# Sliding attention with bias and sink in VectorE's extreme pass, and a last stage that weighs four row tiles on TensorE

## The chip, the cores and the metric

One NeuronCore of a Trainium2 chip runs the kernel; the other cores do nothing for it. The metric is the device time of one execution in microseconds. Engines by name: TensorE (PE, with its weight loads PEld), VectorE (DVE), ScalarE (ACT), GpSimd (POOL) and SyncE (SP), which issues most of the transfers.

## The reference

It computes one inference step of a one-layer encoder on 1024 prompt rows and 64 sample rows of width 1024, all in fp32. Cut to what matters here:

```python
def sink_attention(q, k, v, bias, sinks):                   # 8 query heads on 2 kv heads, 64 wide
    sc = einsum(q, k) * SCALE + bias                        # bias: -slope * |distance|, -inf outside the window
    m = maximum(max(sc, axis=-1), sink)
    e = exp(sc - m[..., None])
    pr = e / (sum(e, axis=-1, keepdims=True) + exp(sink - m)[..., None])
    return einsum(pr, v)

q_a, k_a, v_a, logf, q_b, k_b, v_b = project(rmsnorm(x))    # one input projection
o_a = forgetting attention (8 heads, causal);  o_b = sliding attention, window of 3 chunks of 64
x = x + concat(rmsnorm(o_a), rmsnorm(o_b)) @ w_out
h = rmsnorm(x)
y = x + sum over the 2 chosen of 32 experts: weight * (silu(h @ w_gate) * (h @ w_up)) @ w_down
return rmsnorm(y, g_final), and the new keys and values
```

## The kernel before

All work is laid out in row tiles of 128: eight of the prompt and one with the 64 sample rows, so NT = 9. Five engines run programs of their own, each in the order written down, and wait on semaphores. The stages follow each other: input projection (to about 254 us of the profiled execution), forgetting attention (260 to 411), sliding attention (412 to 500), output projection with routing (504 to 655), experts (660 to 872), last stage (872 to the end). fp32 products of the attention's scores and of the projections are made of three products of rounded parts (high and low halves).

**Sliding attention.** 36 steps n, nine tiles i for each of four groups g; a step handles one query tile of two heads (u = 0, 1) against up to two key tiles. TensorE's order in step n is: transposes of the probabilities n (`strans`), scores n+2 (`sqk`), weighted values n-1 (`spv`). `sqk` first writes the distance bias into the bank by a product of the identity with a bf16 table (`alibi`), and the sink's value into column 256 by a product of ones with a column that holds it in three bf16 parts; the score products accumulate on top. VectorE's order in a step is: copy of half of the transposed probabilities (`scopy`), extreme of n+2 (`smax`, one reduction over two heads and the sink column), scaling of output n-1 (`snorm`, reciprocal and product), then in some steps the low halves of the next group's queries (`s_low_q`) and of one eighth of w_out (L1282). ScalarE's order is: exponentials of n+1 read from PSUM (`sexp`), the other half of the copy, then in some steps the high halves of queries and w_out. GpSimd is idle here. A bank of scores is free for n+2 when the exponentials of n are done.

**Last stage.** When the last expert's rows lie in DRAM (`experts_done`), SP loads the final gain and then, for each of nine tiles, two 128x1024 blocks of expert rows (ya, yb; four slots). VectorE adds both with their weights to the residual in `o_all` (L1538, L1541), ScalarE makes the square sum and root (`norm_f`), VectorE the reciprocal and scaled output (`scale_f`, L1546, L1548) into one of two buffers (`fin`), and SP stores it. VectorE's order is add 0, add 1, scale 0, add 2, scale 1 and so on. SP's is: loads 0 to 3, then per tile i the load of i+4 (when add i is done) and the store of i. TensorE is idle, and GpSimd too.

Of the kernel before, what the change touches and what calls it, by code (L numbers as in the profile page):

```python
# [15 lines left out]
P = 128  # L16
D = 1024
# [28 lines left out]
def build(nc, t):  # L46

    ctx = ExitStack()
    with ctx:
# [52 lines left out]
        assert at + 8 * P <= free0 + 7 * D  # L102
# [34 lines left out]
        for name in ("den", "pg", "inv", "e21"):  # L137
# [6 lines left out]
        fin = [cut(big, free0 + 7 * D + u * D, D) for u in range(2)]  # L144
# [24 lines left out]

        ya = [cut(fox, 2 * WSLOT + u * D, D) for u in range(4)]  # L170
# [97 lines left out]
        sink_r = sinkp[:, 0:NH]  # L268
        sink_b, sink_1, sink_2 = (sinkp[:, NH + n * NH // 2:NH + (n + 1) * NH // 2].bitcast(BF16) for n in range(3))
# [31 lines left out]
            r_step r_exp r_mask r_mm r_id r_slot r_hot r_table id_init id_in v_ids  # L301
            pool_went idx_set dst_set g_done gT_done gT_cs gT_cv gu_done e_done ev_step hid_done hidT_done hidT_cp dn_done y_cs y_cv hg_set
            v_idx v_g v_w v_gT v_gTc v_gu v_e v_s v_hid v_hT v_hTc v_dn v_y v_out experts_done
            f_acc f_stat f_rms f_rstd f_fin f_out_a f_out_b""".split()
# [8 lines left out]
        y_in = [sem(f"y_in{u}") for u in range(4)]  # L313
# [65 lines left out]
        def scaled(g):  # L379

            return SCALE if g in (5, 6) else 1.0
# [13 lines left out]
        S_AT = {3: 0, 6: 1}  # L395
# [18 lines left out]
        def _(sp):  # L414
# [127 lines left out]
            sp.wait_ge(s["r_id"], 1)  # L542
# [55 lines left out]
            sp.dma_start(g1[:, :], row(t["g_final"], D)).then_inc(s["g_late_in"], 16)  # L598
# [5 lines left out]
            def store(i, u):  # L604
                sp.wait_ge(s["f_fin"], i + 1)
                sp.dma_start(t["y_prompt"].rearrange("a s d -> (a s) d")[ds(i * P, P), :], fin[u]).then_inc(s["f_out_b" if u else "f_out_a"], 16)
# [3 lines left out]
            for i in range(NT):  # L610
                if i + 4 < NT:
                    sp.wait_ge(s["f_acc"], i * 2 + 2)
                    load_y(i + 4, i % 4, P if i + 4 < SAMPLE else DEC)
                if i < SAMPLE:
                    store(i, i % 2)
            sp.wait_ge(s["f_fin"], NT)
            sp.dma_start(t["y_sample"].rearrange("a s d -> (a s) d"), fin[0][0:DEC, :]).then_inc(s["f_out_a"], 16)
            sp.wait_ge(s["f_out_a"], 16 * 5)
            sp.wait_ge(s["f_out_b"], 16 * 4)

        @block.gpsimd
        def _(pool):
# [22 lines left out]
            pool.iota(slots, [[1, P]], base=0, channel_multiplier=0, allow_small_or_imprecise_dtypes=True).then_inc(s["r_slot"], 1)  # L645
# [92 lines left out]
        def _(act):  # L738
# [141 lines left out]
            def s_high_q(g, part):  # L880

                a, b = PARTS[part]
                if g >= 2:
                    act.wait_ge(s["s_qk"], (g - 1) * NT)
                act.activation(sqh[g % 2][:, a:b, :], sq_raw[:, g, a:b, :], ACT.Copy, scale=SCALE).then_inc(s["s_hi"], 1)

            for n, (first, end) in enumerate(S_KEYS):
                s_high_k(n, first, end, 4 + n)
                if n < 2:
                    s_high_q(0, n)  # L890

            def sexp(n):
                lo = P if n % NT == 0 else 0
                act.wait_ge(s["s_nm"], n + 1)
# [17 lines left out]
            for n in range(NW):  # L912
# [4 lines left out]
                if i in S_AT and g < 3:  # L917
                    s_high_q(g + 1, S_AT[i])
# [101 lines left out]


# [15 lines left out]
            def norm_f(i, u, rows):  # L1037
                act.wait_ge(s["f_acc"], i * 2 + 2)
                if not (isinstance(i, int) and i < 2):
                    act.wait_ge(s["f_out_b" if u else "f_out_a"], (i - u) * 8)  # L1040
                act.activation(fin[u][0:rows, :], o_all[0:rows, ds(i, 1), :].rearrange("p a n -> p (a n)"), ACT.Square,
                               accum_out=st[0:rows, u:u + 1]).then_inc(s["f_stat"], 1)
                act.wait_ge(s["f_stat"], i + 1)
                act.activation(st[0:rows, 2 + u:3 + u], st[0:rows, u:u + 1], ACT.Sqrt, bias=eps[0:rows, 0:1], scale=1.0 / D).then_inc(s["f_rms"], 1)

            norm_f(0, 0, P)
            norm_f(1, 1, P)
            with act.Fori(1, NP_T // 2) as j:
                for u in range(2):
                    norm_f(j * 2 + u, u, P)  # L1050
            norm_f(8, 0, DEC)

        @block.vector
        def _(dve):
# [107 lines left out]
            def sink_step(n, ins):  # L1162
                ins.then_inc(s["s_aug"], 1)
                dve.wait_ge(s["s_aug"], n)

            pairs = sraw[:, :].rearrange("p (v g) -> p g v", v=2)
            by_pair = [a_.rearrange("p (g v) -> p g v", v=2) for a_ in (sink_1, sink_2, sink_r, sink_b)]
            sink_step(1, dve.tensor_copy(by_pair[0], pairs))
            sink_step(2, dve.tensor_tensor(by_pair[2], pairs, by_pair[0], ALU.subtract))
            sink_step(3, dve.tensor_copy(sink_2, sink_r))  # L1170
            sink_step(4, dve.tensor_tensor(sink_r, sink_r, sink_2, ALU.subtract))
            sink_step(5, dve.tensor_scalar(sink_b, sink_1, ident[:, 0:1], None, ALU.mult))
            sink_step(6, dve.scalar_tensor_tensor(out=sink_b, in0=sink_2, scalar=ident[:, 1:2], in1=sink_b, op0=ALU.mult, op1=ALU.add))
            sink_step(7, dve.scalar_tensor_tensor(out=sink_b, in0=sink_r, scalar=ident[:, 2:3], in1=sink_b, op0=ALU.mult, op1=ALU.add))

# [55 lines left out]
            def s_low_q(g, part):  # L1231

                a, b = PARTS[part]
                dve.wait_ge(s["s_hi"], sided(g, part))
                dve.scalar_tensor_tensor(out=sq_l[:, g, a:b, :], in0=sq_raw[:, g, a:b, :], scalar=SCALE, in1=sqh[g % 2][:, a:b, :].bitcast(F32),
                                         op0=ALU.mult, op1=ALU.subtract).then_inc(s["s_lo"], 1)

            for n, (first, end) in enumerate(S_KEYS):
                s_low_k(n, first, end, 4 + n)
                if n < 2:  # L1240
                    s_low_q(0, n)
# [28 lines left out]
            for n in range(NW):  # L1270
# [6 lines left out]
                if i in S_AT and g < 3:  # L1277
                    s_low_q(g + 1, S_AT[i])
                if n in WO_AT:
                    c = WO_AT.index(n)  # L1280
                    dve.wait_ge(s["wo_hi_set"], c + 1)
                    dve.tensor_tensor(w_out_l[:, c, :], fox[:, c * D + w_out_at:(c + 1) * D + w_out_at], w_out_h[:, c, :].bitcast(F32),  # L1282
                                      ALU.subtract).then_inc(s["wo_lo_set"], 1)
# [750 lines left out]
```

## Time and profile before

| | |
|---|---|
| time, median of 3 runs | 981.83 us (920.51, 981.83, 982.62) |
| the profiled execution: its own time, its span | 920.88 us, 919.0 us |
| mean granted TensorE clock | 0.940 |
| busy share PE, PEld, DVE, ACT, POOL | 87%, 75%, 49%, 36%, 12% |
| mean DMA rate | 136 GB/s |

The span runs from the first to the last instruction of the profiled execution; times of rows are microseconds from its start. Busy shares are means over stages with different limits, so each stage is read by itself.

### The profile page before, as it was taken

Reading aid. Unit: us, or ns where it says so; the run is one execution under the profiler, and the core shown is the slowest. Engines: PE = TensorE matmul, PEld = TensorE weight load, DVE = VectorE, ACT = ScalarE, POOL = GpSimd, SP = SyncE. Lnnn points to the kernel's source line nnn. Section 1 sums busy time; section 2 is a strip of 40 time slices with the busy share of each in tenths; the row PEclk is TensorE's granted clock in tenths of the full one; section 3 lists DMA queues with packets and bytes.
Section 4 is the critical chain, followed back from the end, with each engine's and each line's share of the span. In section 5 each row is a group of like instructions: output and inputs, shape, how many; then the busy total and the mean of one; then the engine's idle time right before and its main releaser. Section 6 shows DMA issues by size and latency. Waiting matters only on the chain.

```text
span 919.0 us, 15046 instructions
## 1 busy us (share of the span) xinstructions
PE 798.8 (87%) x5519; PEld 690.5 (75%) x5519; DVE 448.6 (49%) x1107; ACT 326.8 (36%) x811; POOL 111.0 (12%) x167
## 2 busy tenths in 40 slices
PE   3999999999969898899997999997499999999600
PEld 3999999999947676678997788886377777777400
DVE  4741111111056566656786447555356544544368
ACT  5631111112146566556775433322122222222123
POOL 0000000000021412000000000001223443343100
PEclk9999999999979999998998899999599999999955
DMA  9211411321350211005002312211699999972196
GB/s 276 72 56 47 139 50 46 69 67 49 82 113 6 61 36 29 1 21 210 2 2 85 149 50 88 69 58 67 222 401 406 362 331 341 336 287 83 47 388 216
DMA packets 68851, 124.63 MB, mean 136 GB/s; under 512 B 21787, under 2 KB 41075, under 8 KB 68787
## 3 DMA queue, kind: packets, MB, share of 16 engines
q1 hardware_dynamic: 59571, 105.91, 33.4%
q0 software_dynamic: 9216, 17.85, 5.3%
q8 instruction: 43, 0.70, 0.3%
q14 instruction: 21, 0.17, 0.1%
HBM read 108.72 MB, written 30.73 MB: 152 GB/s over the span
## 4 chain that ended last, share of the span: by engine, by line
PE 74%; DVE 9%; DMA 7%; ACT 5%; issue 3%; SPq 1%; POOLq 0%; DVEq 0%; ACTq 0%
PE ps L1580 30%; PE ps L1909 11%; PE ps L1915 5%; PE ps L1793 4%; PE ps L1686 4%; PE ps L1670 4%; PE ps L1902 3%; PE ps L1769 2%; DMA work<-c_rows 2%; ACT big L837 2%; PE ps L1701 2%; PE ps L1780 2%; DMA work<-in_w_in 2%; PE ps L1848 2%; DVE big L1186 1%
## 5 line engine op out<-in xcount | busy, mean ns | idle before, releaser
L1580 PE MATMUL ps<-xh,wg_lo 128*128 128x384 f32 (+1 forms) x288 | 94.7, 329 | 0.0
L1580 PE MATMUL ps<-xh,wg_hi 128*128 128x384 f32 (+1 forms) x288 | 93.9, 326 | 0.0
L1580 PE MATMUL ps<-xl,wg_hi 128*128 128x384 f32 (+1 forms) x288 | 93.8, 326 | 0.0
L1909 PEld LDWEIGHTS ps<-fox,work 128*128 128x128 f32 x320 | 60.6, 190 | 19.5 <-issue 12.3
L1909 PE MATMUL ps<-fox,work 128*128 128x256 f32 x320 | 72.5, 379 | 2.1 <-DVE work L1478 2.1
L1478 DVE COPY work<-ps 128x512 f32<-128x512 f32 x32 | 22.1, 692 | 91.6 <-PE ps L1902 91.5
L1686 PE MATMUL ps<-cf,big 128*128 128x128 f32 x312 | 49.6, 285 | 16.9 <-ACT big L837 15.3
L1580 PE MATMUL ps<-w_out_h,oTl 128*128 128x512 f32 x144 | 58.5, 407 | 1.5 <-DVE oTl L1321 1.5
L837 ACT ACTIVATE big<-big,nm 128x384 f32<-128x384 f32 (+7 forms) x72 | 54.1, 753 | 11.1 <-DVE nm L1186 10.8
L1081 DVE TENSOR_SCALAR fox<-ps 128x256 f32<-128x256 f32 (+2 forms) x21 | 10.2, 486 | 96.8 <-PE ps L1580 96.8
L1580 PE MATMUL ps<-w_out_h,oTh 128*128 128x512 f32 x144 | 56.8, 395 | 0.0
L1580 PE MATMUL ps<-w_out_l,oTh 128*128 128x512 f32 x144 | 56.8, 394 | 0.0
L1686 PEld LDWEIGHTS ps<-cf,big 128*128 128x128 f32 x312 | 35.3, 143 | 26.4 <-ACT big L837 21.5
L1580 PEld LDWEIGHTS ps<-xl,wg_hi 128*128 128x128 f32 x288 | 54.1, 188 | 0.0
L1580 PEld LDWEIGHTS ps<-xh,wg_lo 128*128 128x128 f32 x288 | 54.1, 188 | 0.0
L1580 PEld LDWEIGHTS ps<-xh,wg_hi 128*128 128x128 f32 x288 | 54.1, 188 | 0.0
L764 ACT ACTIVATE fox<-ps 128x256 f32<-128x256 f32 (+2 forms) x21 | 9.2, 436 | 96.7 <-PE ps L1580 96.7
L984 ACT ACTIVATE big<-ps 128x128 f32<-128x128 f32 x32 | 8.9, 277 | 96.7 <-PE ps L1909 96.7
L900 ACT ACTIVATE big<-ps,nm 128x257 f32<-128x257 f32 (+1 forms) x72 | 32.7, 461 | 24.5 <-DVE nm L1248 24.5
L1580 PE MATMUL ps<-wg_hi,xl 128*128 128x256 f32 x144 | 40.9, 284 | 0.2 <-DVE wg_lo L1077 0.2
L1580 PE MATMUL ps<-wg_lo,xh 128*128 128x256 f32 x144 | 40.8, 283 | 0.0
L1580 PE MATMUL ps<-wg_hi,xh 128*128 128x256 f32 x144 | 40.8, 283 | 0.0
(313 smaller groups left out, 1879.2 us busy)
## 6 DMA issues: line engine op xcount, KB each, us to landing
fox<-in_w_gate SPq DMA_DIRECT2D x20, 512.0 KB, 5.1
fox<-in_w_up SPq DMA_DIRECT2D x20, 512.0 KB, 12.2
fox<-in_w_down SPq DMA_DIRECT2D x20, 512.0 KB, 12.6
fox<-y_rows SPq DMA_DIRECT2D x16, 512.0 KB, 6.4
work<-in_w_in SPq DMA_DIRECT2D x6, 1024.0 KB, 5.6
h_rows<-big SPq DMA_DIRECT2D x9, 512.0 KB, 2.6
work<-in_x_prompt SPq DMA_DIRECT2D x8, 512.0 KB, 4.4
fox<-in_w_out SPq DMA_DIRECT2D x1, 4096.0 KB, 13.4
```

Source lines behind the costliest of these rows:

```text
L837: act.activation(prob[u][:, 0:w], prob[u][:, 0:w], ACT.Exp, bias=nm[:, 2 * (n % 2) + u:2 * (n % 2) + u + 1], scale=-1.0, accum_out=rs[:, 2 ...
L900: act.activation(sprob[n % 2][:, u, lo:2 * P + 1], ps[n % 2][:, 512 * u + lo:512 * u + 2 * P + 1], ACT.Exp, bias=nm[:, 2 * (n % 2) + u:1 + ...
L1478: dve.tensor_copy(hgT[u][:, 4:8, :], bank[1].rearrange("p (c k) -> p c k", c=4)).then_inc(s["gT_cv"], 1)
L1580: mm = pe.matmul(out, xs[a](c), ws[b](c), start=(c + k == 0), stop=(c == C - 1 and k == 2))
L1670: mm = pe.matmul(ps[u][:, at_:at_ + (m1 - m0) * P], q, key, start=(k == 0 and at_ // 512 != own // 512), stop=(k == 2), skip_group_check=True)
L1686: mm = pe.transpose(bank[b][:, (m % 4) * P:(m % 4) * P + P], prob[u][:, m * P:(m + 1) * P], ident)
L1701: mm = pe.matmul(bank[6][u * DH:u * DH + DH, 0:P], v, probT[u][n % 2][:, b * P:(b + 1) * P], start=(b == 0), stop=(b == nblk[i] - 1), skip ...
L1769: mm = pe.matmul(bank[2 * (n % 2) + u][:, at_:at_ + (m1 - m0) * P], q, key, start=False, stop=(k == 2), skip_group_check=True)
L1793: mm = pe.matmul(bank[6][:, (n % 2) * P + v * DH:(n % 2) * P + (v + 1) * DH], sprobT[n % 2][:, (2 * v + b) * P:(2 * v + b + 1) * P], val, ...
L1902: mm = pe.transpose(bank[c // 4][:, (c % 4) * P:(c % 4) * P + P], src[:, c, :], ident)
L1909: mm = pe.matmul(bank[2 + u][:, 0:2 * FE].rearrange("p (m f) -> p m f", m=2), hgT[u][:, c, :], wv[:, c, :, :], start=(c == 0), stop=(c == ...
L1915: mm = pe.matmul(bank[4 + n], ex["hidT"][u], w[:, 2 * D + 512 * n:2 * D + 512 * n + 512], start=True, stop=True)
```

## The change

In the sliding stage, `sqk` no longer puts bias and sink into the bank; the scores alone are made there. `smax` becomes two passes, one per head, each of which computes -(score + bias) into a buffer of SBUF (`sscore`) and, in the same pass, its minimum with the negated sink. `sexp` reads this buffer with scale -1, one head at a time; the sink is a column of it, copied in the first two steps of each group. A bank is free after the passes. Queries are scaled where they leave the projection. Halves of the queries of groups 1 to 3 and w_out's low halves move to GpSimd. In the last stage, tiles 1, 3, 5 and 7 are weighed on TensorE: diagonal matrices of the weights times ya and yb are summed in PSUM and VectorE adds the result once. Outputs have four buffers, squares one of their own, and the final gain is loaded while the experts run. SP waits with a slot's next load until the matmuls have read it.

```diff
+        squares = cut(swa, 0, D)
+        ON_PE = [1, 3, 5, 7]
+        diag = cut(swa, 5 * D, 2 * len(ON_PE), P)
+        fin = [cut(swa, D + u * D, D) for u in range(4)]
...
-        S_AT = {3: 0, 6: 1}
+        S_AT = {1: 0, 3: 1}
...
             gate_up(NSLOT, 0)
+            sp.wait_ge(s["hT_done"], 2 * NT)
+            sp.wait_ge(s["h_out_a"], 16 * 5)
+            sp.wait_ge(s["h_out_b"], 16 * 4)
+            sp.dma_start(g_fin, row(t["g_final"], D)).then_inc(s["g_late_in"], 16)
...
             for i in range(NT):
                 if i + 4 < NT:
-                    sp.wait_ge(s["f_acc"], i * 2 + 2)
+                    if i in ON_PE:
+                        sp.wait_ge(s["f_mm"], ON_PE.index(i) + 1)
+                    else:
+                        sp.wait_ge(s["f_acc"], i * 2 + 2)
                     load_y(i + 4, i % 4, P if i + 4 < SAMPLE else DEC)
+                store(i)
...
+            def side_piece(g, part):
+                a, b = PARTS[part]
+                hi = sqh[g % 2][:, a:b, :]
+                pool.tensor_copy(hi, sq_raw[:, g, a:b, :]).then_inc(s["s_hi"], 1)
+                pool.wait_ge(s["s_hi"], sided(g, part))
+                pool.tensor_tensor(sq_l[:, g, a:b, :], sq_raw[:, g, a:b, :], hi.bitcast(F32), ALU.subtract).then_inc(s["s_lo"], 1)
+            def low_out(c):
+                pool.wait_ge(s["wo_hi_set"], c + 1)
+                pool.tensor_tensor(w_out_l[:, c, :], fox[:, c * D + w_out_at:(c + 1) * D + w_out_at], w_out_h[:, c, :].bitcast(F32),
+                                   ALU.subtract).then_inc(s["wo_lo_set"], 1)
+            for n in range(NW):
+                g, i = n // NT, n % NT
+                if i in S_AT and g < 3:
+                    pool.wait_ge(s["s_qk"], n + 1)
+                    side_piece(g + 1, S_AT[i])
+                if n in WO_AT:
+                    low_out(WO_AT.index(n))
...
-                act.wait_ge(s["s_nm"], n + 1)
                 for u in range(2):
-                    act.activation(sprob[n % 2][:, u, lo:2 * P + 1], ps[n % 2][:, 512 * u + lo:512 * u + 2 * P + 1], ACT.Exp,
-                                   bias=nm[:, 2 * (n % 2) + u:1 + 2 * (n % 2) + u],
+                    act.wait_ge(s["s_nm"], 2 * n + u + 1)
+                    act.activation(sprob[n % 2][:, u, lo:2 * P + 1], sscore[n % 2][:, u, lo:2 * P + 1], ACT.Exp,
+                                   bias=nm[:, 2 * (n % 2) + u:1 + 2 * (n % 2) + u], scale=-1.0,
...
+            for k, i in enumerate(ON_PE):
+                for c in range(2):
+                    last = act.activation(diag[:, 2 * k + c, :], ident, ACT.Copy, scale=wgt[:, c * NT + i:c * NT + i + 1])
+                last.then_inc(s["f_diag"], 1)
...
-                dve.tensor_reduce(nm[:, 2 * (n % 2):2 * (n % 2) + 2], ps[n % 2][:, :].rearrange("p (u n) -> p u n", u=2)[:, :, lo:2 * P + 1],
-                                  AX.X, ALU.max, negate=True).then_inc(s["s_nm"], 1)
+                if i < 2:
+                    dve.tensor_copy(sscore[n % 2][:, :, 2 * P], neg_sink[:, 2 * g:2 * g + 2])
+                for u in range(2):
+                    a0 = g * 512 + u * 256
+                    dve.tensor_tensor_reduce(sscore[n % 2][:, u, lo:2 * P], bank[2 * (n % 2) + u][:, lo:2 * P], alibi[:, a0 + lo:a0 + 2 * P],
+                                             -1.0, neg_sink[:, 2 * g + u:2 * g + u + 1], ALU.add, ALU.min,
+                                             nm[:, 2 * (n % 2) + u:2 * (n % 2) + u + 1]).then_inc(s["s_nm"], 1)
...
             def add_y(i, j, u, rows):
+                if i in ON_PE:
+                    k = ON_PE.index(i)
+                    dve.wait_ge(s["f_mm"], k + 1)
+                    dve.tensor_tensor(o_all[0:rows, i, :], ps[k][0:rows, :], o_all[0:rows, i, :], ALU.add).then_inc(s["f_acc"], 2)
+                    return
...
                 if n >= 2:
-                    pe.wait_ge(s["s_exp"], 2 * (n - 1))
+                    pe.wait_ge(s["s_nm"], 2 * (n - 1))
-                for u in range(2):
-                    out = bank[2 * (n % 2) + u]
-                    a0 = g * 512 + u * 256
-                    pe.matmul(out[:, lo:2 * P], identb, alibi[:, a0 + lo:a0 + 2 * P], start=True, stop=False, skip_group_check=True)
-                for u in range(2):
-                    pe.matmul(bank[2 * (n % 2) + u][:, 2 * P:2 * P + 1], onesb, sink_b[:, 2 * g + u:2 * g + u + 1],
-                              start=False, stop=False, skip_group_check=True)
...
+            def weigh_y(k, i):
+                pe.wait_ge(s["f_diag"], k + 1)
+                pe.wait_ge(y_in[i % 4], Y_BASE[i % 4] + i // 4 * 32 + 32)
+                for n in range(2):
+                    cols = slice(512 * n, 512 * n + 512)
+                    pe.matmul(ps[k][:, cols], diag[:, 2 * k, :], ya[i % 4][:, cols], start=True, stop=False)
+                    mm = pe.matmul(ps[k][:, cols], diag[:, 2 * k + 1, :], yb[i % 4][:, cols], start=False, stop=True)
+                mm.then_inc(s["f_mm"], 1)
+            for k, i in enumerate(ON_PE):
+                weigh_y(k, i)
```

The seven small instructions that split the sinks into bf16 parts (L1168 to L1174, before the forgetting attention) become one that negates them.

## Rows read from the trace of the kernel before

**Rows 1.** The page: chain that ended last, share of the span by engine.

```profile
PE 74%; DVE 9%; DMA 7%; ACT 5%; issue 3%; SPq 1%; POOLq 0%; DVEq 0%; ACTq 0%
```

**Rows 2.** Chain of waits, 408 to 506 us: shares by line; one step (start us, us, what).

```profile
by line: PE ps L1793 36.4%; PE ps L1769 21.5%; PE ps L1780 16.5%; PE ps L1753 8.3%; PE ps L1817 2.0%; PE ps L1701 1.9%; DVE skl L1228 1.5%; DVE big L1296 1.5%; issue 1.4%; DVE sq_l L1235 1.4%; PE ps L1734 1.1%; PE ps L1755 1.0%; PE ps L1710
...
447.51 0.44 PE ps L1780 x4
447.95 0.22 PE ps L1753 x2
448.20 0.55 PE ps L1769 x6
448.75 1.03 PE ps L1793 x8
```

**Rows 3.** Groups of the sliding stage, 416 to 499 us.

```profile
L1248 DVE TENSOR_REDUCE nm<-ps 128x2 f32<-128x514 f32 x32 | 22.1, 690 | 12.3 <-PE ps L1769 12.3
...
L1256 DVE COPY big<-ps 128x256 f32<-128x256 f32 x32 | 13.3, 416 | 0.0
...
L1265 DVE TENSOR_TENSOR big<-ps,rc 128x128 f32<-128x128 f32 x35 | 10.2, 292 | 9.5 <-PE ps L1793 9.0
L1282 DVE TENSOR_TENSOR w_out_l<-fox,w_out_h 128x1024 fp32r<-128x1024 f32 x8 | 9.7, 1216 | 0.0
...
L1261 DVE RECIPROCAL rc<-rs 128x2 f32<-128x2 f32 x36 | 5.6, 155 | 0.0
```

**Rows 4.** Busy time of 440 to 452 us: PE, PEld, DVE, ACT, POOL; clock, DMA share, GB/s.

```profile
440.00:452.00 12.00, 12.00 (x117) 11.03 (x116) 9.96 (x26) 8.86 (x29) 0.00 (x0) 1.00 0.00 1
```

**Rows 5.** Groups of VectorE in the forgetting attention (260 to 411 us), and of GpSimd.

```profile
L1186 DVE CUSTOM_DVE_ANT_0 big<-ps,work 128x1024 f32<-128x1024 f32 x4 | 4.9, 1220 | 2.7 <-PE ps L1670 2.7
...
L1186 DVE CUSTOM_DVE_ANT_0 big<-ps,work 128x256 f32<-128x256 f32 x4 | 1.7, 422 | 1.3 <-PE ps L1670 1.2
...
L635 POOL TENSOR_TENSOR q_l<-fox,qh 128x640 fp32r<-128x640 f32 x3 | 4.7, 1550 | 0.2
...
L635 POOL TENSOR_TENSOR q_l<-fox,qh 128x512 fp32r<-128x512 f32 x3 | 3.8, 1272 | 0.2
```

**Rows 6.** Chain of waits, last stage (868 us to the end).

```profile
872.18 0.34 SPq L598
...
873.04 6.15 DMA fox<-y_rows
...
879.30 1.30 DVE big L1538
...
886.27 1.21 DVE big L1538
...
888.90 1.29 DVE big L1548
890.19 1.21 DVE big L1538
...
914.38 1.28 DVE big L1548
```

**Rows 7.** Busy time by stretch, last stage; last columns: granted clock, DMA share, GB/s.

```profile
868.00:872.00 4.00, 0.00 (x0) 0.00 (x0) 0.00 (x0) 0.00 (x0) 0.86 (x1) 0.66 0.15 57
...
876.00:878.00 2.00, 0.00 (x0) 0.00 (x0) 0.00 (x0) 0.00 (x0) 0.00 (x0) 0.50 1.00 410
...
902.00:904.00 2.00, 0.00 (x0) 0.00 (x0) 1.96 (x2) 0.98 (x2) 0.00 (x0) 0.50 1.01 262
```

**Rows 8.** Chain of waits: routing's end and the experts' start.

```profile
644.85 3.62 PE ps L1848 x16
...
664.93 8.43 PE ps L1909 x32
...
674.35 1.72 PE ps L1915 x4
676.07 3.45 PE ps L1909 x16
```

More of the change, by code:

```diff
@@ L101, in build @@
         sprobT = [cut(big, at + u * 4 * P, 4 * P) for u in range(2)]
-        assert at + 8 * P <= free0 + 7 * D
+        at += 8 * P
+        sscore = [cut(big, at + u * 2 * (2 * P + 8), 2, 2 * P + 8) for u in range(2)]
+        at += 4 * (2 * P + 8)
+        assert at <= free0 + 7 * D
         xr = [cut(big, free0 + u * D, D) for u in range(2)]
@@ L142, in build @@
         assert at <= free0 + 6 * D
-        fin = [cut(big, free0 + 7 * D + u * D, D) for u in range(2)]
+        g_fin = cut(big, free0 + 2 * D, D)
         fox, fox_at = sb_at("fox", [P, NT * QKV + WSLOT])
@@ L267, in build @@
         sinkp = sb("sinkp", [P, 4 * NH])
-        sink_r = sinkp[:, 0:NH]
-        sink_b, sink_1, sink_2 = (sinkp[:, NH + n * NH // 2:NH + (n + 1) * NH // 2].bitcast(BF16) for n in range(3))
+        neg_sink = sinkp[:, 0:NH]
         sraw = sb("sraw", [P, NH])
@@ L312, in build @@
         y_out = [sem(f"y_out{u}") for u in range(4)]
-        y_in = [sem(f"y_in{u}") for u in range(4)]
+        f_out = [sem(f"f_out{u}") for u in range(4)]
+        y_in, Y_BASE = x_in, [48, 32, 32, 32]
         x_rows = t["x_prompt"].rearrange("a s d -> (a s) d")
@@ L602, in load_y, with store @@
                 sp.dma_start(yb[u][0:rows, :], y_dram[ds(i * P + TOK, rows), :]).then_inc(y_in[u], 16)
-            def store(i, u):
+            def store(i):
+                rows = t["y_prompt"].rearrange("a s d -> (a s) d")[i * P:(i + 1) * P, :] if i < SAMPLE else t["y_sample"].rearrange("a s d -> (a s) d")
                 sp.wait_ge(s["f_fin"], i + 1)
-                sp.dma_start(t["y_prompt"].rearrange("a s d -> (a s) d")[ds(i * P, P), :], fin[u]).then_inc(s["f_out_b" if u else "f_out_a"], 16)
+                sp.dma_start(rows, fin[i % 4][0:P if i < SAMPLE else DEC, :]).then_inc(f_out[i % 4], 16)
             for i in range(4):
@@ L611, in _ @@
                 if i + 4 < NT:
-                    sp.wait_ge(s["f_acc"], i * 2 + 2)
+                    if i in ON_PE:
+                        sp.wait_ge(s["f_mm"], ON_PE.index(i) + 1)
+                    else:
+                        sp.wait_ge(s["f_acc"], i * 2 + 2)
                     load_y(i + 4, i % 4, P if i + 4 < SAMPLE else DEC)
[L614 to L619, printed above, removed]
+                store(i)
+            for u in range(4):
+                sp.wait_ge(f_out[u], 16 * len(range(u, NT, 4)))
         @block.gpsimd
@@ L1034, in _, with norm_f @@
             act.wait_ge(s["experts_done"], 1)
-            def norm_f(i, u, rows):
+            def norm_f(i):
+                u, rows = i % 2, P if i < SAMPLE else DEC
                 act.wait_ge(s["f_acc"], i * 2 + 2)
[L1039 to L1042, printed above, removed]
+                act.activation(squares[0:rows, :], o_all[0:rows, i, :], ACT.Square, accum_out=st[0:rows, u:u + 1]).then_inc(s["f_stat"], 1)
                 act.wait_ge(s["f_stat"], i + 1)
+                if i >= 2:
+                    act.wait_ge(s["f_rstd"], i - 1)
                 act.activation(st[0:rows, 2 + u:3 + u], st[0:rows, u:u + 1], ACT.Sqrt, bias=eps[0:rows, 0:1], scale=1.0 / D).then_inc(s["f_rms"], 1)
-            norm_f(0, 0, P)
-            norm_f(1, 1, P)
-            with act.Fori(1, NP_T // 2) as j:
-                for u in range(2):
-                    norm_f(j * 2 + u, u, P)
-            norm_f(8, 0, DEC)
+            norm_f(0)
+            for i in range(NT):
+                if i + 1 < NT:
+                    norm_f(i + 1)
         @block.vector
@@ L1160, in _ @@
                 flow(piece)
[L1162 to L1174, printed above, removed]
+            dve.tensor_scalar(neg_sink.rearrange("p (g v) -> p g v", v=2), sraw[:, :].rearrange("p (v g) -> p g v", v=2), -1.0, None,
+                              ALU.mult).then_inc(s["s_aug"], 1)
             def fmax(n, u):
@@ L1276, in _ @@
                     snorm(n - 1)
[L1277 to L1283, printed above, removed]
             snorm(NW - 1)
@@ L1768, in sqk @@
                                 key = swa_h[rows, m0:m1, 0:P]
-                            mm = pe.matmul(bank[2 * (n % 2) + u][:, at_:at_ + (m1 - m0) * P], q, key, start=False, stop=(k == 2),
-                                           skip_group_check=True)
+                            mm = pe.matmul(bank[2 * (n % 2) + u][:, at_:at_ + (m1 - m0) * P], q, key,
+                                           start=(k == 0 and at_ == spans[0][0]), stop=(k == 2), skip_group_check=True)
                 mm.then_inc(s["s_qk"], 1)
```

52 lines of the change are left out of this document (24 added, 28 removed).

## The prediction

> **What bounds the kernel now.** I read the chain of waits of the whole span first [rows 1]: TensorE holds 74% of it and VectorE 9%. The change touches two stages, so I read each by itself. The sliding stage runs from 411.75 to 499.7 us. Its chain [rows 2] is TensorE alone: one of its 36 steps is 0.44 us of transposes (L1780), 0.22 of bias (L1753), 0.03 of sink (L1755, seen only in the row by line), 0.55 of scores (L1769) and 1.03 of weighted values (L1793), 2.27 us in all, and a window of it has TensorE busy 12.00 of 12.00 us at full clock, VectorE 9.96 and ScalarE 8.86 [rows 4]. So here only what leaves TensorE shortens anything. In the last stage TensorE does nothing and VectorE runs without a gap: two weighted sums and a scaling per tile, 3.91 us from one tile to the next (886.27 to 890.19), first sum at 879.30, last scaling from 914.38 to 915.66 [rows 6]. But the DMA engines are full too, 410 GB/s from 876 us on and still saturated at 902 to 904 [rows 7]. A saving on VectorE there has little room before transfers end last.
>
> **Sliding stage: bias and sink leave TensorE.** By the row by line, L1753 holds 8.3% and L1755 1.0% of the 98 us window [rows 2]: 8.1 + 1.0 = 9.1 us, all on the path. The sink's one-column products overlap their neighbours, so their price is the 0.03 us a step, not their durations. Score matmuls stay as they are. A step becomes 2.27 - 0.25 = 2.02 us.
>
> Cover for this is VectorE. Each step had one 128x514 reduction, 0.69 us [rows 3]; now it has two 128x256 passes that add bf16 bias to PSUM and take the extreme. The nearest row is the forgetting attention's pass of that size, 0.42 us [rows 5], there with an fp32 second input. So a step of VectorE is 0.42 (copy) + 2 x 0.42 + 0.16 (reciprocal) + 0.29 (scaling of output) [rows 3] = 1.71 us, under 2.02 even before the overlap that back-to-back instructions show. The eight low-half subtractions of 1.22 us (L1282) leave its queue as well. Nothing late is created in order either: VectorE's order is copy n, extreme n+2, scaling n-1. With time 0 at a step's first transpose, scores n+2 end at 0.99, passes at 1.9, scaling n-1 at 2.4; TensorE asks for that scaling only at 3.0. Exponentials n+2 start after the first pass, at 1.5, take 2 x (0.47 + 0.2), and are wanted at 4.04. ScalarE loses its query halves and keeps w_out's high halves. It now reads scores from SBUF instead of PSUM, and a score bank is free after the pass instead of after the exponential; both only loosen. Bounds of this edit: if a pass with the bf16 input costs 0.42 us, -9.1 us. With overlap of the first steps, which run at half clock and where bias costs 0.43 us and the exponential waits less, another -1. If it cost up to 0.57 us, still the full gain. I take -9.5 us, bounds -11 and +5 (first rival).
>
> GpSimd takes what left the others: per group two casts and subtractions (1.27 us for 128x512, 1.55 for 128x640 [rows 5]) and eight 128x1024 subtractions. From those rows each further 128 columns cost 0.28 us, so 128x1024 is an estimated 2.4 us. Queries of the next group begin at step 1 of a group and are wanted at step 7, 12 us later, with at most two 2.4 us subtractions queued in front; the last w_out piece follows step 29, 12 us before the output projection wants it. Cost nothing; if that cover were gone, a late piece would stop TensorE for its 2.4 us.
> Eight small VectorE copies of the sink column are SBUF to SBUF. The Trainium skill (SBUF — State Buffer, section "SBUF: two separate sides") says that a VectorE copy in a two-port mode and a GpSimd instruction exclude each other for a whole instruction. No row of before shows such a pair; by it each copy that meets a w_out subtraction would wait up to an estimated 2.4 us. Six of the eight stand where GpSimd waits for the same scores or has finished, so I leave the sum as it is.
> Seven small sink instructions before the first forgetting pass vanish; the pass waits for the c_rows transfer anyway. Nothing. The earlier load of the final gain (0.5 MB) enters SP's queue behind an expert whose successors are loaded seven experts ahead, and its added waits are for stores that end before gathers start. Nothing.
>
> **Last stage.** Three effects, each against before's 879.30.
> (a) Gain not loaded here: SP's issue of 872.18 is gone and the rows' is 0.39 us earlier, and 0.5 MB less ahead of the first tile at 410 GB/s, 1.3 us. First sum at 877.6: -1.7 us.
> (b) Four tiles need one add from PSUM, by the nearest row (the extreme pass of 128x1024, 1.22 us, or L1538's 1.21) about 1.2 us, in place of 2.48: -1.28 each, -5.1 us in all. Floor of VectorE's work: 9 x 1.43 + 5 x 2.48 + 4 x 1.2 = 30.1 us instead of 35.2.
> (c) What TensorE needs. Tile 1's rows land one tile's 1.05 MB after tile 0's, 2.56 us, at 880.1, just when VectorE ends tile 0. Weighing is four fp32 matmuls of 512 columns. L1915 has two in 1.72 us at full clock [rows 8], so 3.45 us. But TensorE has been idle since 866; the window 868 to 872 already has 0.66 and the later ones 0.50 [rows 7], the 1.2 GHz level, where it is 6.9 us. How soon does the clock come back? The burst L1848 of 3.62 us stayed at half; at the expert stage's start 32 matmuls took 8.43 us where two times 3.45 is full speed, 1.53 us more, so it rose 3.1 us into them and 7.8 after the first transpose [rows 8]. Between those I take 6.1 us, bounds 5.0 and 6.9. In VectorE's order this add stands before tile 0's scaling, so tiles 0 and 1 are both held: +6.1 us.
> Behind it SP's order bites: it issues tile 5's load only after store 0, that is after tile 0's scaling at 888.9. Store and load are 1.5 MB, 3.8 us, plus some 2 us of latency: tile 5 lands at 895, TensorE is cold again (4.5 us idle; the mean of 0.66 puts the earlier drop at 869.3, 3 us after the last matmul), weighs until 900.4 to 901.9, and VectorE wants it at 899.3: +1.8 us. Tiles 3 and 7 are in time (890 against 892.8; 906 against 907.7). The final scaling waits as before.
> Sum: 877.6 + 30.1 + 6.1 + 1.8 + 0.5 for the last statistics = 916.1 against 915.7: +0.4 us; bounds -3 and +3. The diagonals (8 ScalarE copies of 128x128) run while the last scatter lands: nothing. Four output buffers instead of two remove ScalarE's waits on stores, which stopped nobody: VectorE has no gap in [rows 6].
>
> **Sum.** The profiled execution took 920.88 us, span 919.0. 920.9 - 9.5 + 0.4 = 911.8 us, 1.0% less. The timed runs shown are 920.51, 981.83 and 982.62; their median lies 61 us above the profiled one, and the profile shows nothing of those 61 us. I carry the difference of 9.1 over to the median: 981.8 - 9.1 = 972.7 us. Two of three runs lie at that level, so a median of three falls there more often than not, about 6 in 10; otherwise it is about 912.
>
> **Rivals**, each as a difference to before and at both levels.
> 1. VectorE becomes the bound of the sliding stage. If the pass with a bf16 bias costs over 0.70 us instead of 0.42, VectorE's step exceeds 2.27 and the stage gets longer than before: the decision point is (2.27 - 0.87)/2. At 0.77 us: 36 x (2.41 - 2.27) = +5, with the last stage +5.4: 926.3, at the median's level 987. For it: no row has this type. Against: fp32 passes and bf16 matter not to the cadence of any VectorE row shown. 8%.
> 2. The last stage keeps its saving, since the clock returns at once and tile 5 is early: +6.1 becomes 3.5 and +1.8 nothing, -4 there: 907.4 or 968. 15%.
> 3. The exclusion of the ports named above decides: say all eight copies wait 2.4 us; a step's slack on VectorE of 0.3 us absorbs little, 8 x 2.1 = +17 us, gain gone: 929 or 990, slower. For it: both engines are now busy together. Against: the order of their triggers, as worked out. 3%.
> 4. The stall in (c) is repeated: TensorE is cold for all four tiles, each late by 2 to 3 us: +6 instead of +0.4: 917.4 or 978, no change by measure. 14%.
> 5. The sliding stage's own waits eat half of its gain (TensorE behind GpSimd or exponentials): -4.5: 917 or 977. 12%.
> My own case: 48%.
>
> **How the numbers follow.** Predicted 972.7. The likeliest case's own range is 969 to 977, or 908 to 916 at the other level. The range must reach over both levels, since the level of the median is not decided by the change: low end 905 (rival 2 at the lower level), high end 982 (rivals 4 and 5 with the bounds of the stage); outside are rivals 1 and 3 and some scatter. 2% (18 us) is about what a measurement here can tell; all cases but rival 3 and the ends lie within it. Faster by over 2% needs the stage's full -11 and the last stage's -7 or more: 8%; slower, rival 3 and mishaps of that size: 7%.
>
> **What would show it.** In the sliding stage's chain no matmul with a bf16 bias, steps of 2.02 us, TensorE still busy throughout, passes near 0.42 us and an end of the stage about 9 us earlier. In the last stage: first sum at some 38.5 us before the end as before, VectorE idle some 6 us before the first PSUM add, a granted clock of 0.5 when TensorE's first weighing starts, store 0 some 2.5 us later than before. Wrong would be: TensorE waiting for the exponential in steady state, or VectorE's adds finding f_mm already set.

## The result, and the profile after

The changed kernel takes 972.77 us, the median of 971.13, 972.04, 973.51 and 974.34. Before takes 920.51, 925.01, 981.83 and 982.62 in the same comparison. Before has two levels of time, some 922 and some 982 us, and the changed kernel was seen on one only; the ratio of 1.054 (1.049 to 1.060) sets it against before's lower level. It is slower there by 5.4%. Against before's upper level it is 1% faster. So the question is what the two levels are, and why the changed kernel was seen on only one of them.

First the page of the changed kernel: the totals, the granted clock by slices of 24.2 us, the chain by engine, two groups.

```profile
span 969.3 us, 14926 instructions
PE 866.9 (89%) x5407; PEld 733.7 (76%) x5407; DVE 441.9 (46%) x1199; ACT 332.7 (34%) x813; POOL 142.1 (15%) x187
...
PEclk9999999999889999965555599999679999999976
...
PE 78%; DVE 7%; DMA 7%; ACT 4%; issue 3%; SPq 1%; POOLq 0%; DVEq 0%; ACTq 0%
...
L1810 PE MATMUL ps<-swa,big 128*128 128x64 f32 x256 | 64.3, 426 | 0.0
...
L1273 DVE CUSTOM_DVE_ANT_0 big<-ps,cb,sinkp 128x256 f32<-128x256 f32 (+1 forms) x72 | 30.9, 466 | 27.8 <-PE ps L1786 27.8
```

The clock row has a hole of six slices (6 5 5 5 5 5), which is the sliding stage from its start to its end. Before's page, profiled at the lower level, has 8 or 9 there:

```profile
PEclk9999999999979999998998899999599999999955
```

The same stage in the chain of waits of the changed kernel, in order of time. L1797 is the transposes (L1780 of before), L1786 the scores (L1769), L1810 the weighted values (L1793):

```profile
by line: PE ps L1810 49.4%; PE ps L1797 28.4%; PE ps L1786 27.7%
...
494.86 0.85 PE ps L1797 x4
495.71 0.94 PE ps L1786 x5
496.65 1.90 PE ps L1810 x8
```

Bias and sink are gone, as intended, and the chain is TensorE alone, as in [rows 2]. But a step takes 0.85 + 0.94 + 1.90 = 3.69 us where I had 2.02 and before had 2.27: each part lasts nearly twice as long as the same part in [rows 2]. The windows tell why; the columns are those of [rows 4], the last three the granted clock, the DMA share and GB/s.

```profile
416.00:420.00 4.00, 2.67 (x17) 1.79 (x16) 3.01 (x15) 2.14 (x9) 1.89 (x2) 0.74 1.03 422
420.00:422.00 2.00, 2.00 (x12) 1.45 (x11) 1.25 (x6) 1.36 (x5) 0.14 (x1) 0.50 1.01 403
422.00:424.00 2.00, 2.00 (x12) 1.67 (x14) 1.52 (x7) 1.37 (x5) 1.92 (x2) 0.50 1.04 414
...
440.00:452.00 12.00, 12.00 (x60) 10.44 (x61) 5.64 (x28) 5.98 (x20) 4.18 (x3) 0.50 0.00 1
```

In [rows 4] TensorE is busy 12.00 of 12.00 us at a granted clock of 1.00 (2.4 GHz); here it is just as busy, at 0.50 (1.2 GHz), with 60 matmuls instead of 117 (before's 117 include the bias and sink products). In both kernels the clock falls near the start of the stage. In the changed kernel it falls at about 417.9 us, behind waits of 1.45 and 1.18 us for the halves of keys and queries. In the profiled execution of before it had fallen at about 411.9 us, during the transposes of the keys, ahead of its waits (0.82 and 0.50 us). There it comes back between two neighbouring microseconds, which no group of rows ahead of the prediction shows:

```profile
421.00:422.00 1.00, 1.00 (x8) 0.83 (x7) 0.28 (x1) 1.00 (x5) 0.00 (x0) 0.50 1.02 410
422.00:423.00 1.00, 1.00 (x11) 0.85 (x10) 0.48 (x1) 0.25 (x1) 0.00 (x0) 0.94 1.03 410
```

In the changed kernel it stays at 0.50 until the output projection. The stage, from the first transpose of the keys to the end of the last scaling, runs from 412.74 to 546.64 us, 133.9 us instead of 87.9 (411.75 to 499.69). The last scaling in the chain of each, first the changed kernel, then before:

```profile
546.34 0.30 DVE big L1291
```

```profile
499.39 0.30 DVE big L1265
```

The last stage, in the timeline of VectorE and TensorE. In brackets stands the idle time before, and what ended it.

```profile
924.45 1.28 DVE L1562 SCALAR_TENSOR_TENSOR big<-fox,wgt,big 128x1024 f32<-128x1024 f32 x1 [10.31 <-DMA fox<-y_rows]
...
932.23 1.23 DVE L1558 TENSOR_TENSOR big<-ps,big 128x1024 f32<-128x1024 f32 x1 [5.18 <-PE ps L2008]
...
938.67 1.22 DVE L1558 TENSOR_TENSOR big<-ps,big 128x1024 f32<-128x1024 f32 x1
...
948.03 1.22 DVE L1558 TENSOR_TENSOR big<-ps,big 128x1024 f32<-128x1024 f32 x1 [2.83 <-PE ps L2008]
...
957.88 1.22 DVE L1558 TENSOR_TENSOR big<-ps,big 128x1024 f32<-128x1024 f32 x1 [3.33 <-PE ps L2008]
```

```profile
927.04 2.05 PE L2007 MATMUL ps<-fox,swa 128*128 128x512 f32 x2 [13.63 <-DMA fox<-y_rows]
...
941.58 2.05 PE L2007 MATMUL ps<-fox,swa 128*128 128x512 f32 x2 [5.74 <-DMA fox<-y_rows]
...
951.04 2.04 PE L2007 MATMUL ps<-fox,swa 128*128 128x512 f32 x2 [3.12 <-DMA fox<-y_rows]
```

VectorE waits three times for the weighing, 11.3 us in all, and TensorE starts tiles 1, 5 and 7 after idle times of 13.6, 5.7 and 3.1 us, each with a first pair of records that takes 2.05 us (a pair at a clock of 1.00 takes 1.02). Tile 3 follows tile 1 without a gap and costs VectorE nothing. From the first load of rows to the end of the last scaling the stage takes 919.40 to 966.00 = 46.6 us; before took 872.18 to 915.66 = 43.5. The books: 1.0 us later start of the sliding stage, 46.0 in it, 0.3 between, 3.1 in the last stage = 50.4 us, against 50.3 between the two profiled executions (971.13 and 920.88).

### The profile page after: what moved, and what is told of

It is laid out like the page before. It is cut to its first block, busy times and chain, and to the rows that moved or that the text cites. A ratio compares the mean times of both kernels' runs of the same rounds, so it can differ in the third digit from the quotient of the medians.

```text
span 969.3 us, 14926 instructions
## 1 busy us (share of the span) xinstructions
PE 866.9 (89%) x5407; PEld 733.7 (76%) x5407; DVE 441.9 (46%) x1199; ACT 332.7 (34%) x813; POOL 142.1 (15%) x187
## 4 chain that ended last, share of the span: by engine, by line
PE 78%; DVE 7%; DMA 7%; ACT 4%; issue 3%; SPq 1%; POOLq 0%; DVEq 0%; ACTq 0%
PE ps L1605 30%; PE ps L1926 11%; PE ps L1810 7%; PE ps L1932 5%; PE ps L1711 4%; PE ps L1786 3%; PE ps L1695 3%; PE ps L1797 3%; PE ps L1919 3%; DMA work<-c_rows 2%; ACT big L870 2%; PE ps L1726 2%; PE ps L1865 2%; DMA fox<-y_rows 2%; DMA work<-in_w_in 1%
## 5 line engine op out<-in xcount | busy, mean ns | idle before, releaser
L1810 PE MATMUL ps<-swa,big 128*128 128x64 f32 x256 | 64.3, 426 | 0.0
L1810 PEld LDWEIGHTS ps<-swa,big 128*128 128x128 f32 x256 | 57.9, 327 | 6.1 <-issue 5.2
L931 ACT ACTIVATE big<-big,nm 128x257 f32<-128x257 f32 (+1 forms) x72 | 35.3, 491 | 35.0 <-DVE nm L1273 34.4
L1273 DVE CUSTOM_DVE_ANT_0 big<-ps,cb,sinkp 128x256 f32<-128x256 f32 (+1 forms) x72 | 30.9, 466 | 27.8 <-PE ps L1786 27.8
```

Of the source, the lines that this page charges most:

```text
L931: act.activation(sprob[n % 2][:, u, lo:2 * P + 1], sscore[n % 2][:, u, lo:2 * P + 1], ACT.Exp, bias=nm[:, 2 * (n % 2) + u:1 + 2 * (n % 2) ...
L1273: dve.tensor_tensor_reduce(sscore[n % 2][:, u, lo:2 * P], bank[2 * (n % 2) + u][:, lo:2 * P], alibi[:, a0 + lo:a0 + 2 * P], -1.0, neg_sink ...
L1810: mm = pe.matmul(bank[6][:, (n % 2) * P + v * DH:(n % 2) * P + (v + 1) * DH], sprobT[n % 2][:, (2 * v + b) * P:(2 * v + b + 1) * P], val, ...
```

## The experiments

Theory A: the two levels are the clock of the sliding stage, which in before mostly comes back at its start and in the changed kernel never, since the two bias products of a step are missing. The rivals: B, the levels are something else and the clock of 0.50 is a second effect; C, a clock that is up is held by the new steps, and only the start is at fault (against the strict form of A, in which the new steps can't hold it); D, chance. The added products read two tables that are there anyway and write bank 7, which nobody reads in this stage: the output is that of the changed kernel.

**Before, unchanged.**

> The kernel before, unchanged. Theory A (the granted TensorE clock of the sliding stage decides between two levels of time, whatever the kernel): its runs split into times near 920 us with a mean granted clock near 0.94 and times near 982 us with a mean clock near 0.88, and nothing between; the 61 us are the sliding stage at 1.2 GHz. Rival B (the 61 us come from elsewhere, transfers for instance): runs near 982 us show the same mean clock of 0.94.

It took 982.83, 924.74, 926.53, 982.97, 922.79 and 920.95 us, and the profiled one was the first, at the upper level. Its clock by slices, and a window:

```profile
PEclk9999999999799999955555589999869999999955
```

```profile
440.00:452.00 12.00, 12.00 (x70) 11.06 (x70) 4.82 (x13) 5.04 (x16) 0.00 (x0) 0.50 0.01 1
```

That is the hole of the changed kernel, in before: its sliding stage runs from 411.86 to 561.3 us, 149.4 instead of 87.9, and those are the 61 us between before's runs. B falls. Its last scaling:

```profile
561.00 0.30 DVE big L1265
```

A step of before costs 0.85 + 0.43 + 0.03 + 0.94 + 1.90 = 4.15 us at this level, so the change saves 0.46 us a step there and not 0.25 (149.4 against 133.9 us for the stage, 15.5 us less); the spans are 981.0 and 969.3 us. Over all comparisons before ran 66 times, 17 of them at the upper level.

The two profiled executions of before differ in one more thing: when the clock falls. First the one at the lower level, then this one.

```profile
408.00:412.00 4.00, 2.66 (x34) 1.87 (x31) 0.91 (x4) 0.55 (x2) 0.00 (x0) 0.99 0.14 15
412.00:416.00 4.00, 3.18 (x20) 2.72 (x18) 2.55 (x5) 2.56 (x6) 0.00 (x0) 0.50 0.90 347
```

```profile
408.00:412.00 4.00, 2.66 (x35) 1.87 (x32) 0.92 (x4) 0.56 (x2) 0.00 (x0) 1.00 0.23 30
412.00:416.00 4.00, 1.96 (x20) 1.58 (x19) 2.81 (x6) 2.56 (x6) 0.00 (x0) 1.00 0.86 332
416.00:420.00 4.00, 3.65 (x23) 2.88 (x24) 1.47 (x6) 2.00 (x9) 0.00 (x0) 0.53 1.03 420
```

Up to 411.9 us TensorE did the same work at the same times within 0.11 us. In one execution the clock fell there and came back at about 422.1 us; in the other it fell at about 416.3 us, behind waits of 1.45 and 0.95 us, and stayed down. So the longer waits of the changed kernel aren't the missing products: this execution has the products and nearly the same waits. Whether an early fall is what sends before to its lower level can't be told from one profile of each. The moment alone doesn't decide it in the variants that follow: with two products back the clock fell at about 415.5 us and came back at 422.4, with one product it fell at 411.7 and stayed down.

**The changed kernel, unchanged, once more.**

> The changed kernel, unchanged. Theory D (the changed kernel has the same two levels as the one before, and its first four runs all fell on the upper one by chance): some runs near 914 us, 1.0% under the lower level of before (9.5 us less in the sliding stage, 3 more in the last), and the others near 972 us. Theory A (without the bias products the clock never rises in the sliding stage): all runs near 972 us.

970.27, 967.26, 970.16, 975.41, 969.91 and 971.68 us, ratio 1.053 (1.049 to 1.056). With the first four runs that is 10 of 10 at the upper level, where before has 17 of 66. D falls.

**Two products a step back.** In every step, ahead of the scores:

```diff
+                for u in range(2):
+                    pe.matmul(bank[7][:, 0:2 * P], identb, alibi[:, u * 256:u * 256 + 2 * P], start=True, stop=True)
```

> The changed kernel plus two products per sliding step of the size of the removed bias products (identity by 128x256 bf16), into a bank that nothing reads. Theory A (the changed stage stays at 1.2 GHz because the removed products were the activity that let the clock rise or stay up): the clock is 2.4 GHz in at least some runs, steps of 2.24 us, span near 921 us, 1.05 times shorter than the changed kernel. Rival C (the clock fails for what happens at the stage's start, not for the steady work): granted clock stays 0.5, steps of 4.1 us, about 985 us.

922.38, 951.11, 980.61 and 920.34 us. In the profiled one, the first, the clock comes back where it did in before:

```profile
420.00:422.00 2.00, 2.00 (x12) 1.71 (x12) 1.19 (x8) 1.28 (x6) 1.05 (x1) 0.50 1.02 420
422.00:424.00 2.00, 2.00 (x18) 1.44 (x16) 1.21 (x6) 1.33 (x6) 0.82 (x2) 0.91 1.02 410
```

Products that compute nothing save some 50 us in two of four runs. The run of 951.11 us has a mean granted clock of 0.918, between the 0.952 of the two short runs and the 0.887 of the long one. One product a step instead of two:

> The changed kernel plus one product of 128x256 bf16 per sliding step, half of what the run with two put back. Theory A (the steady share of products decides how often the clock rises): between none of the runs (no product) and most of them (two products) at 2.4 GHz; those near 916 us, the others near 977. If it were the length of TensorE's step or the moment of the start alone, no run or all runs would be up.

Three of nine runs came out at 915.1 to 917.3 us, six at 973.4 to 981.3. That is more than without a product (none of 10 runs of the changed kernel). Between one product and two (2 or 3 of 4) so few runs can't tell a difference.

**Transposes in place of the products**, two fp32 transposes of 128x128 a step into bank 7:

> The changed kernel plus two transposes of 128x128 fp32 per sliding step, of the same time on TensorE as the two bf16 products of the run before, into a bank that nothing reads. If any busy TensorE time counts for the clock, it behaves as the run with products (2.4 GHz in some runs, about 921 us). If transposes do not count: 0.5 throughout, step 3.69 + 0.43 = 4.1 us, about 985 us.

985.3 once, the profiled run, and ten times 919.5 to 928.3; ratio of the ten 1.0025 (1.0001 to 1.0048). The profiled run has the clock at 0.50 through the stage, as the changed kernel. Transposes serve as well as products, so it need not be bias products that bring the clock back. Whether they do more than two products (10 of 11 against 2 or 3 of 4) these runs can't tell.

**A burst at the start of the stage**, before the first scores:

```diff
+            for r in range(20):
+                pe.matmul(bank[7], identb, alibi[:, 0:512], start=True, stop=True)
```

> The changed kernel plus 20 products of 128x512 bf16 once, at the start of the sliding stage behind the transposes of the keys, where TensorE waits for the split keys and queries (4.3 us at full clock, of which at most 3 lie on the path); nothing reads their result. Rival C (start decides, and the steady work of the changed stage holds a clock that is up): 2.4 GHz throughout, steps of 2.02 us, span near 913 us. Theory A in its strict form (steady work without the bias products cannot hold the clock): it falls back to 0.5 within some us and the span is near 970 us.

Seven of ten runs at 915.5 to 920.1 us (ratio 0.996, 0.994 to 0.998), three at 973.7 to 977.4. The profiled one is of the three:

```profile
416.00:420.00 4.00, 4.00 (x17) 1.70 (x16) 1.81 (x5) 0.73 (x3) 0.00 (x0) 0.83 1.02 416
420.00:424.00 4.00, 3.21 (x26) 1.77 (x24) 2.48 (x14) 2.13 (x9) 1.89 (x2) 1.00 1.02 412
424.00:428.00 4.00, 3.85 (x20) 2.99 (x22) 2.51 (x12) 2.78 (x11) 2.09 (x2) 0.52 0.77 296
```

The clock had fallen at about 413.9 us; it comes back at 417.3 during the burst and stays at 1.00 up to about 424.1 us. In the first steps behind the burst TensorE waits again, 0.65 us of it for exponentials (3.21 busy of 4.00), the clock falls, and the steady steps that follow do not raise it. By their times the seven faster runs got past this place; none of them was profiled.

**The burst two steps later**, behind the last wait of the start:

```diff
                 strans(n)
+                if n == 2:
+                    for r in range(24):
+                        pe.matmul(bank[7], identb, alibi[:, 0:512], start=True, stop=True)
```

> The changed kernel plus 24 products of 128x512 bf16 once, behind the transposes of sliding step 2, when all later steps are steady work; nothing reads them. Theory C (the clock is lost in the sparse start, and steady steps hold a clock that is up but cannot raise one that is down): the burst raises it, all runs stay at 2.4 GHz behind it, all near 918 to 921 us (914 plus 5 to 7 us for the burst), none near 972. Theory A in its strict form (steady steps cannot hold it): some or all fall back to 0.5.

Twelve of twelve at 919.8 to 925.3 us, ratio 1.0004 (0.9987 to 1.0020). The chain of waits from the burst on, and then two windows:

```profile
423.24 5.75 PE ps L1821 x24
428.99 0.55 PE ps L1786 x6
...
432.61 0.44 PE ps L1797 x4
433.05 0.55 PE ps L1786 x6
433.60 1.03 PE ps L1810 x8
```

```profile
424.00:428.00 4.00, 4.00 (x20) 1.74 (x19) 0.00 (x0) 0.00 (x0) 0.00 (x0) 0.97 0.50 184
440.00:452.00 12.00, 12.00 (x108) 10.19 (x108) 9.77 (x47) 9.66 (x32) 7.33 (x6) 1.00 0.01 2
```

C holds, and the strict form of A falls: once the clock is up (here at about 424.3 us, during the burst), the steps of the changed kernel hold it to the end of the stage, 69 us. A step is 0.44 + 0.55 + 1.03 = 2.02 us. The burst gives back 5.75 us of what it brings.

**The changed kernel without the weighing on TensorE.** All nine tiles are summed on VectorE as before; the early load of the gain and the four output buffers stay.

```diff
-            for k, i in enumerate(ON_PE):
-                weigh_y(k, i)
...
-                if i in ON_PE:
-                    k = ON_PE.index(i)
-                    dve.wait_ge(s["f_mm"], k + 1)
-                    dve.tensor_tensor(o_all[0:rows, i, :], ps[k][0:rows, :], o_all[0:rows, i, :], ALU.add).then_inc(s["f_acc"], 2)
-                    return
```

> The changed kernel with all nine tiles of the last stage weighed on VectorE, as before; the early load of the final gain and the four output buffers stay, so do all changes of the sliding stage. If the last stage lost by the waits for TensorE, it takes 41.5 us from the first row load to the last store's issue instead of 46.6, 5 us less, at either clock level of the sliding stage. If TensorE's part only took the place of other waits (transfers), it stays near 46.

965.77, 967.88, 967.68 and 966.14 us; span 963.4 against 968.4 of the changed kernel on that chip. All four at the upper level: the last stage has no part in it. The chain of waits:

```profile
919.06 0.34 SPq L611
...
924.14 1.30 DVE big L1550
...
958.80 1.28 DVE swa L1562
```

The stage takes 919.06 to 960.08 = 41.0 us. So the +3.1 us of the change's last stage are -2.5 for the early gain and the four output buffers together (43.5 to 41.0) and +5.6 for the weighing (41.0 to 46.6).

**A version with both**: no weighing, 20 products at the start and 12 at step 2.

> The changed kernel, all tiles of the last stage weighed on VectorE, plus 20 products of 128x512 bf16 where TensorE waits at the start of the sliding stage and 12 more behind the transposes of step 2; nothing reads them. Theory C: the first keep the clock up through most of the sparse start, the second carry it into the steady steps, all runs at 2.4 GHz and near 914 us (the early burst alone ran at 916.3 in its runs at 2.4 GHz; 12 x 0.22 = 2.6 us more, 5 us less in the last stage). If the clock is lost in spite of both, runs near 970.

Six of six at 912.1 to 914.5 us, median 913.45, ratio 0.990 (0.987 to 0.993): faster than before's lower level by 1.0%, than the changed kernel by 6%. In the profiled run the clock is 1.00 from 404 us to the end of the stage, though TensorE waits 0.66 and 0.23 us for exponentials behind the first burst, as it did where the run with the early burst alone lost the clock; so these waits alone don't explain that loss. And before with the same two bursts:

> The kernel before plus the same two bursts. Theory C: the upper level near 982 us is gone; all runs near 922 to 925 us (12 x 0.22 = 2.6 us for the second burst, up to 1 for the first). The distance to the run with two bursts in the changed kernel is what the sliding stage and the early gain really give: 9.5 us there and 2 in the last stage, 1.2%. If before's upper level had another cause, it stays.

Eleven of twelve at 924.1 to 928.9 us, none near 982; the twelfth took 1655.88 us, which is neither level (its mean granted clock is given as 1.0), and of which there is no profile. Ratio 1.0038 (1.0021 to 1.0055). The bursts take before's upper level away too. The first burst and the end of the sliding stage in the chains of both, first the version, then before with bursts:

```profile
413.35 4.26 PE ps L1751 x19
...
492.72 1.09 PE ps L1801 x8
...
493.90 0.30 DVE big L1284
```

```profile
414.13 4.84 PE ps L1739 x19
...
502.14 1.09 PE ps L1796 x8
...
503.32 0.30 DVE big L1265
```

From the first transpose (411.98 and 411.67) to the end of the last scaling that is 82.2 and 91.95 us: -9.7 us. Not all of it is the edit. In before with bursts the clock had fallen again at about 411.9 us and came back at 415.3, in the version it never fell; so the part up to the end of the first burst took 7.3 us there and 5.6 here. Behind the burst, where both run at 1.00, it is 84.7 against 76.6 us: -8.1 us.

## Why the prediction was wrong, by its steps

**The failed step** is the one under "Sliding stage: bias and sink leave TensorE" that takes 2.02 us a step for granted. The parts were read from a window at full clock [rows 4], and the text even says that the first steps run at half clock, but it never asks what brings the clock back and whether the removed products were part of that. It holds instead that "the level of the median is not decided by the change". With the products the clock came back at 422 us in the profiled execution, and 49 of 66 runs were at the lower level; without them none of 14 was, the four without weighing among them. The steps cost 3.69 us instead of 2.02: 36 x 1.67 = 60 us. The stage grew by 46.0 us where I had -9.5, 55.5 us apart; that is less than 60, as some of the first steps run at 0.50 in before too.

**The second failure is beside it**: "the profile shows nothing of those 61 us". They are the sliding stage at half clock, 36 x (4.15 - 2.27) = 68 us by the steps and 61.5 measured, for the same reason. The profile could have led there: the stage's first row at 0.50 in an otherwise warm stage of 88 us that is all TensorE showed that there was a level to come back from, and the step at half clock could be worked out. That the predicted 972.7 stands near the measured 972.77 is luck: it was carried to the upper level because two of three timed runs lay there, and at that level the stage gives 15.5 us and not 9.5, the last stage +3.1 and not +0.4. As a forecast of the change's sign against the level that before mostly has, it was wrong.

**The size of the edit at equal clock** was nearly right: -9.5 us predicted, of which 9.1 are the products and the rest the first steps; -8.1 us behind the first burst, where both kernels with bursts run at 1.00. TensorE's waits of 0.66 and 0.23 us for exponentials, in the first steps of the version, are part of what is missing. The -9.7 us of the whole stage lie nearer by luck, since before with bursts started it at 0.50.

**VectorE's pass** (rival 1, over 0.70 us needed): 0.48 us for 128x256, 0.466 in the mean of both sizes, against 0.42 taken. Not the bound. GpSimd's 128x1024 subtraction was put at 2.4 us from the slope of [rows 5]; the eight took 2.35, and TensorE was busy 12.00 of 12.00 us beside them. The exponentials did not only loosen by the new source: read from SBUF, 128x257 took 0.503 us in the mean against 0.473 from PSUM in before. It cost nothing, as TensorE waits for none in the steady steps.

**The ports** (rival 3): the eight sink copies lasted 0.160 to 0.171 us each. The Trainium skill (SBUF — State Buffer, section "SBUF: two separate sides") lets a VectorE copy in a two-port mode and a GpSimd instruction exclude each other. No run here tests that: seven of the eight copies meet no GpSimd instruction (the one at 447.21 us ends 0.3 us before a subtraction starts), and the one at 417.89 us overlaps by 0.14 us with a cast that started after it. The rival was answered by the order of the triggers, as argued, and not by the ports.

**Waits eating the gain** (rival 5): none in the steady steps, whose chain has only the three TensorE lines, at 0.50 as at 1.00 (12.00 of 12.00 us busy with the late burst).

**The last stage.** (a) First sum 5.05 us after the first load instead of 7.12: -2.07, predicted -1.7. (b) The add from PSUM took 1.22 us, predicted 1.2. (c) Tile 1: the weighing took 5.1 us at a clock that started at 0.50 and rose (927.04 to 932.1), predicted 6.1, and its rows landed 2.6 us after tile 0's, as predicted; VectorE's wait was 5.2. Tile 5: +2.8, predicted +1.8. Tile 7 was predicted in time and cost 3.3 us: after 3.1 us of idle time TensorE started it at 0.50 again. So the stage is +3.1, a hair outside its bounds of -3 and +3, and between my own case and rival 4 (cold for all four tiles; here for three). Against my terms that is -0.4 for the first sum, -0.9, +1.0 and +3.3 for tiles 1, 5 and 7. The term that was mis-sized is tile 7's, put at nothing; the mechanism is the forecast one, and tile 5's wait was half as long again as forecast.

The Trainium skill (TensorE: Matmul & The Clock Gate, section "What's actually happening") lets sustained busy time of TensorE bring its clock to 2.4 GHz. The window of 440 to 452 us above differs: 12.00 of 12.00 us busy, and the windows from 420 to 440 us as full, at 1.2 GHz; the measurement decides.

**What stays open.** That the clock of the sliding stage makes the levels, that in the profiled executions it is settled within some 12 us of the stage's start, and that added matmuls there bring it back, is shown by putting them in and taking them out. Why the steps with two bias products bring the lower level in 49 of 66 runs, and those without in none of 14, is not: one product helped in 3 of 9 runs, two in 2 or 3 of 4, transposes in 10 of 11, and each of these changed the number of matmuls, their columns and the spacing of the others at once. A rival that no run separates from them is the moment at which the clock falls: in before it fell at 411.9 us in the execution at the lower level and at 416.3 in the one at the upper, after the same work, and nothing here says why. The three profiled executions with the changed sliding stage and nothing added had it fall at 417.9, 415.6 and 417.5 us, so none shows what an early fall does without products. The run of 951.11 us is between the levels in its time and in its mean clock; that the clock came back there in mid-stage fits, but it was not profiled. The 1655.88 us have no explanation here.

## What to carry to other kernels

Before counting a matmul that leaves TensorE as a gain, look at the granted clock where the stage starts, and at what TensorE does there: work that seems to cost 0.25 us a step may be what brings the clock back for 36 steps. Where a kernel's runs fall on two levels, profile one of each before predicting anything, and compare the clock by slices; a stage that is all TensorE and sits behind a stall is the suspect. A short burst of products that nobody reads, behind the last stall (24 of 512 columns, 5.75 us), removed the upper level in 12 of 12 runs. Two bursts (20 of them at the stage's start, 12 at step 2), with the sliding edit kept and the weighing left out, gave the fastest version.

## What the runs showed of the hardware that was not expected

TensorE can be busy without a gap for 120 us and stay at a granted clock of 0.50, as these windows of the changed kernel show (with those of 420 to 424 and 440 to 452 us above), and the same steps keep 1.00 when they start from there, as behind the late burst:

```profile
424.00:440.00 16.00, 16.00 (x85) 13.66 (x84) 6.82 (x29) 6.01 (x21) 0.20 (x1) 0.50 0.15 58
452.00:520.00 68.00, 68.00 (x342) 57.88 (x342) 31.52 (x138) 32.77 (x102) 20.36 (x12) 0.50 0.00 1
520.00:540.00 20.00, 20.00 (x104) 17.27 (x102) 9.16 (x38) 9.19 (x30) 2.35 (x1) 0.50 0.00 1
```

In before the clock fell at 411.9 us with no idle time of TensorE longer than 0.58 us in the 4 us ahead (2.66 of 4.00 us busy from 408 to 412), and in another execution the same work left it at 1.00. In the last stage 3.1 us of idle time were enough to start the next weighing at 0.50; four fp32 matmuls with 512 columns then took 5.1 to 6.8 us where [rows 8] give 3.45 at full clock.
